# A hybrid encoder with 2 x 32 experts on one core: TensorE's order in the experts changed so that a down product stands behind the next expert's gate and up product

## What is computed

```python
def run(args):
    xe, e_i = args
    hdn = jax.nn.silu(xe @ w_gate[e_i]) * (xe @ w_up[e_i])
    return hdn @ w_down[e_i]
...
contrib = yb[dest].astype(F32) * sg[:, None]
return jnp.zeros((T, d), F32).at[stok].add(contrib).astype(xt.dtype)
```

## Time and profile before

| | |
|---|---|
| median of 3 runs | 1803.88 us (1802.73 to 1806.07) |
| profiled execution: its time, its span | 1805.69 us, 1803.8 us |
| TensorE busy | 1589.4 us (88%) |
| VectorE, ScalarE, POOL busy | 695.3, 435.6, 194.1 us |
| granted TensorE clock, mean | 0.973 |
| experts of layer 0, first gate and up product to last down product | 411.2 to 896.7 us |
| experts of layer 1, the same | 1287.0 to 1775.3 us |

### The profile page before, as it was taken

One profiled execution on the slowest core, in us unless ns is written; L12 is line 12 of the kernel. 1 busy time (PEld: TensorE's weight loads), 2 busy tenths in 40 slices (PEclk: granted clock), 3 DMA queues, 4 the chain that ended last, 5 costly groups with the idle time before them and its releaser, 6 DMA issues.

```text
span 1803.8 us, 22591 instructions
## 1 busy us (share of the span) xinstructions
PE 1589.4 (88%) x7494; PEld 763.4 (42%) x7494; DVE 695.3 (39%) x1432; ACT 435.6 (24%) x989; POOL 194.1 (11%) x199
## 2 busy tenths in 40 slices
PE   5999998998998998787889999999899988887883
PEld 2455645453333343333345555455333333333331
DVE  1677576352222112222157855743422222222124
ACT  2111567112111112111121016742111221111111
POOL 0000022111111011111000002101111111111010
PEclk9999999989999999999999999999999999999997
DMA  9625533079999999999972355212799999999994
GB/s 362 231 70 202 195 115 110 17 293 398 407 401 407 408 408 404 417 410 417 365 298 93 122 204 208 68 48 101 290 400 407 403 409 406 411 416 404 399 395 180
DMA packets 118493, 527.56 MB, mean 292 GB/s; under 512 B 16529, under 2 KB 22673, under 8 KB 69265
## 3 DMA queue, kind: packets, MB, share of 16 engines
q1 hardware_dynamic: 100944, 491.49, 69.0%
q0 software_dynamic: 12496, 24.51, 4.2%
q10 hardware_dynamic: 4976, 10.55, 1.6%
HBM read 520.99 MB, written 23.86 MB: 302 GB/s over the span
## 4 chain that ended last, share of the span: by engine, by line
PE 56%; DMA 27%; SPq 6%; DVE 5%; issue 3%; ACT 3%; POOL 1%; ACTq 0%; DVEq 0%; POOLq 0%
DMA ring<-in_w_exp_up 20%; PE ps L1015 18%; PE ps L1373 17%; PE ps L1228 6%; SPq L841 5%; PE ps L1371 4%; DMA hT<-in_w_exp_up 3%; PE ps L1170 2%; PE ps L1184 2%; PE ps L1210 2%; PE ps L1041 1%; DMA ring<-in_w_in 1%; ACT arena L1664 1%; DMA yexp_d<-arena,masks 1%; PE ps L1404 1%
## 5 line engine op out<-in xcount | busy, mean ns | idle before, releaser
L1373 PE MATMUL ps<-ring,arena 128*64 128x512 f32 x1952 | 589.1, 603 | 59.2 <-ACT arena L1664 35.0
L1373 PEld LDWEIGHTS ps<-ring,arena 128*64 128x64 f32 x1952 | 184.8, 138 | 273.5 <-issue 260.2
L1015 PE MATMUL ps<-ring,hT 128*128 128x512 f32 (+1 forms) x768 | 255.0, 487 | 1.5 <-DVE z L1804 0.9
L733 DVE TENSOR_TENSOR arena<-ps,arena 64x512 f32<-64x512 f32 (+1 forms) x64 | 44.3, 693 | 488.6 <-ACT arena L1658 418.6
L1658 ACT ACTIVATE arena<-ps 128x512 f32<-128x512 f32 x64 | 38.2, 597 | 778.9 <-PE ps L1373 724.3
L1015 PEld LDWEIGHTS ps<-ring,hT 128*128 128x128 f32 x768 | 144.4, 191 | 101.5 <-issue 91.2
L1373 PE MATMUL ps<-home,arena 128*64 128x512 f32 x320 | 148.6, 619 | 24.2 <-DMA ring<-in_w_exp_up 20.5
L1373 PE MATMUL ps<-hT,arena 128*64 128x512 f32 x336 | 151.5, 605 | 6.9 <-DMA ring<-in_w_exp_up 6.9
L980 POOL DMA_INDIRECT yexp_d<-arena,masks x64 | 59.3, 927 | 850.3 <-DVE arena L743 772.9
L741 DVE TENSOR_TENSOR arena<-ps,gate 64x512 f32<-64x512 f32 (+1 forms) x64 | 43.7, 683 | 266.2 <-PE ps L1373 246.6
L1228 PE MATMUL ps<-ring,hT 128*128 128x512 f32 x256 | 112.5, 595 | 0.0
(11 more groups left out here) (218 smaller groups left out, 1645.2 us busy)
## 6 DMA issues: line engine op xcount, KB each, us to landing
ring<-in_w_exp_up SPq DMA_DIRECT2D x108, 1024.0 KB
ring<-in_w_exp_down SPq DMA_DIRECT2D x88, 1024.0 KB
ring<-in_w_exp_gate SPq DMA_DIRECT2D x62, 1024.0 KB
ring<-in_w_ada SPq DMA_DIRECT2D x24, 2048.0 KB, 11.1
home<-in_w_exp_gate SPq DMA_DIRECT2D x44, 1024.0 KB
work<-in_w_exp_down SPq DMA_DIRECT2D x40, 1024.0 KB
hT<-in_w_exp_gate SPq DMA_DIRECT2D x22, 1024.0 KB
hT<-in_w_exp_up SPq DMA_DIRECT2D x20, 1024.0 KB
```

What stands on the lines that cost most here:

```text
L1015: last = pe.matmul(out, lhs(k), rhs(k), start=(k == 0), stop=(k == n - 1))
L1373: last = [pe.matmul(outs[c][HALF * c:HALF * c + HALF, :], lhs(k)[:, 0:HALF], rhs(c, k), start=(k == 0), stop=(k == n - 1), tile_position=( ...
```

## The change

On TensorE, the body of the loop was: turned product rows of k, down product of k, gate and up product of k+1, turned tokens of k+2. It becomes: gate and up product of k+1, turned tokens of k+2, down product of k, turned product rows of k+1. On VectorE, the scaling of the down product's rows of k moves behind the tokens of k+2.

```diff
@@ experts_dve
             expert_tokens(0, 0)
             expert_hidden(0, 0, 0)
             expert_tokens(1, 1)
-            expert_rows(0, 0, 0)
             expert_hidden(1, 0, 1)
             expert_tokens(2, 0)
-            expert_rows(1, 0, 1)
+            expert_rows(0, 0, 0)
             expert_hidden(2, 1, 0)
             expert_tokens(3, 1)
+            expert_rows(1, 0, 1)
             with dve.Fori(1, HE - 1) as it:
-                expert_rows(2 * it, it, 0)
                 expert_hidden(2 * it + 1, it, 1)
                 expert_tokens(2 * it + 2, 0)
-                expert_rows(2 * it + 1, it, 1)
+                expert_rows(2 * it, it, 0)
                 expert_hidden(2 * it + 2, it + 1, 0)
                 expert_tokens(2 * it + 3, 1)
+                expert_rows(2 * it + 1, it, 1)
@@ TensorE
                 gate_up(0, 0)
                 turn_tokens(0, 1)
+                turn_hidden(0, 0)
                 with pe.Fori(0, NE // 6) as q:
                     for n in range(6):
-                        turn_hidden(q, n)
-                        down(q, n)
                         gate_up(q, n + 1)
                         turn_tokens(q, n + 2)
-                turn_hidden(NE // 6, 0)
+                        down(q, n)
+                        turn_hidden(q, n + 1)
                 gate_up(NE // 6, 1)
                 down(NE // 6, 0)
```

## The result

The changed kernel takes 1986.78 us in the median of 4 runs (1981.56 to 1991.38), against 1804.62 us (1802.73 to 1806.07, 4 runs) for the kernel before: a ratio of 1.1005, with a 95% interval of 1.0978 to 1.1033. The forecast was slower, 1928 us, with a range of 1864 to 1966: the direction and the loop that causes it hold, the size is 59 us too small and outside the range.

What follows compares the result with a forecast made beforehand. Before, weights bound at 15.7 us per expert, with TensorE's 13.7 us pace early in each stage; after, a gather loop of 16.0 us. 1803.9 + 61.5 (loop, wide experts, stage ends) + 62 (clock) gave about 1928 us, range 1864 to 1966.

Steps and rivals of the forecast that it cites:

- step 2: Expert loop: tokens gathered behind the scatter come late, TensorE waits 3.2 us each step, giving 16.0 us per expert.
- F + 3.55: POOL's issue of the gather three experts ahead, 3.55 us after F, the end of an expert's down product.
- step 6: TensorE's clock falls after three quarters of the gather waits, 1.5 us each over 55 loops: 62 us, bounds 0 and 83.
- step 2's 7.5 us: Time from the gather's issue to its rows landing with DMA engines full, taken from the old order's 7.4 and 7.5.
- work costed at nothing: VectorE's later row scaling and SP's down places freed 8 us later, claimed free since weights come three experts early.
- the wide experts: Three experts, two in layer 0 and one in layer 1, with longer products: some 9 us extra each.
- A: Rival: gather in time, DMA stream sets the end, late release costs +5 to +12 us, 1809 to 1816; chance 0.08.
- B: Rival: gathers land within 4.3 us, quicker steps put more places in flight earlier, 8 us faster, 1796; chance 0.04.
- D: Rival: the gather loop is longer still, a 9 us landing adding 87 us, over 1970; chance 0.08.

Runs made afterwards that it cites:

- e7: Changed kernel with only SP's weight loads reordered, gate and up of the next expert ahead of down of this one; 1901.49 us, ratio 1.0546.
- e2: Changed kernel plus four products of constants on TensorE between the gate and up product and the turned tokens; 1909.99 us, ratio 1.0602.
- e9: Changed kernel with SP's loads as in e7 and the filler of e2, with three products of constants instead of four; 1873.81 us, ratio 1.0376.
- e1: Changed kernel with POOL issuing the gather three experts ahead before the scatter instead of behind it; 1816.14 us, ratio 1.0071.
- e3: Changed kernel with the down product ahead of the turned tokens, and VectorE's scaled rows moved ahead likewise; 1817.11 us, ratio 1.0079.
- e10: Kernel before, TensorE and VectorE in old order, with POOL's gather of two experts ahead put behind the scatter; 2046.97 us, ratio 1.1317.
- e4: Changed kernel with each weight load after the first nine cut to a quarter of its half, timing only; 1695.2 us, one run.
- e5: Kernel before with each weight load after the first nine cut to a quarter of its half, timing only; 1733.57 us, one run.
- e6: Changed kernel with the gather ahead of the scatter as in e1 and SP's loads in TensorE's new order; 1803.75 us, ratio 0.9999.
- e8: Kernel before with only POOL's edit of e1, the gather three experts ahead issued before the scatter; 1802.27 us, ratio 0.9982.

## Why the prediction was right in kind and too small in size

The table has means over those narrow steps in which TensorE waited for the gather, in us, worked out from the timeline rows of TensorE and POOL (51 steps of the changed kernel, 449.24 to 1927.37; 51 of e7; 40 of e2; 46 of e9).

| | forecast | changed | e7 | e2 | e9 |
|---|---|---|---|---|---|
| gather's issue to turned tokens | 7.64 | 8.20 | 7.05 | 8.64 | 7.82 |
| turned tokens | 1.16 | 1.82 | 1.53 | 1.15 | 1.15 |
| down product | 3.65 | 5.03 | 4.66 | 3.65 | 3.69 |
| wait ahead of the turned tokens | 3.2 | 4.07 | 2.93 | 0.88 | 0.94 |
| steps with a slow down product | 3 in 4 | 51 of 51 | 39 of 51 | 0 of 40 | 1 of 46 |

**The loop (step 2).** Right, and shown, with a step of 18.6 us where I had said 16 to 17.5. It closes through down product, scaled rows, scatter, gather, turned tokens: F + 3.55 for the issue is what the timeline after has, 54 waits stand at L1352, and each way of opening the loop (e1, e3) gives 1816 to 1817 us. e10 makes it without the change.

**The clock (step 6).** This is the step that failed, the term that was mis-sized. I took three waits in four to be followed by the low level, at 1.5 us each, 62 us. The granted clock was 0.50 in the stretch from 504 to 508, and 0.86 over 450 to 570, where I had said 0.90 to 0.96. The down product was slow in all 51 steps and the turned tokens in 47 of them, in the mean by 1.38 + 0.66 = 2.04 us: 51 x 2.04 = 104 us, 42 more than forecast. Both factors were too low. My 1.5 came from one gate and up product behind a wait of 2.46 us. My share came from the waits of the kernel before, and it was too low even for a wait of the size that I forecast. In the changed kernel the 7 waits of 1.74 to 3.3 us were all followed by the low level, like the 44 longer ones. In e7, 10 of the 11 waits of 3.0 to 3.3 us were, and all 17 longer ones. That e7 comes to 39 of 51, close to my three in four, is the work of its short waits: of the 17 under 2.5 us only 7 were. Length alone doesn't decide it: in the kernel before, TensorE kept its clock behind the wait of 3.04 us in the earlier trace rows.

**The landing (step 2's 7.5 us).** This is the second term that was mis-sized: 8.20 us to the turned tokens instead of 7.64, 0.56 x 51 = 29 us. I took the landing from the old order as a constant, although I had seen it go from 3.8 to 10.8. e7 shows that it depends on the order of the loads around it. Under "work costed at nothing" I wrote that the later release of places costs nothing here, since the weights come early; the weights did, but all five halves went out at the moment of the gather. e7 shows what that was worth: with the loads moved, landings are 1.15 us shorter to the turned tokens and the whole kernel 85 us faster, by way of the clock as well.

**The rest.** The 58 steps from the first to the 30th scatter of each layer last 541.7 and 539.5 us, 18.6 each; the forecast's were (482 + 473 + 62) / 58 = 17.5. The two terms above come to 71 us over the forecast and this difference to 64. By the ends of the down products in the timeline, the 51 narrow steps that waited lasted 18.5 us in the mean, 72 over the forecast's 17.1. The other seven (three with a wide gate and up product, 18.9 each; three with a wide down product, 21.7 to 22.8; the last of layer 1) lasted 135.8 us where I had charged 143.5. More than half of this difference is that last step: it took 12.4 us and waited for no gather. The rest is the wide experts, which I overcharged a little.

Two of my readings were loose, and neither moves the forecast. The DMA line stands at 9 from the tenth slice on, not from the ninth (7, 293 GB/s). And 1803.9 + 61.5 gives 1865 for the lower end of the range, not 1864.

**The rivals.** A's price, 5 to 12 us, was a microsecond too low for e1 (13), but A needs a landing of at most 4.3 us, and the median here was 8.1. The rule of the Trainium skill for a transfer from GpSimd (DMA: Bandwidth & Descriptors, Anatomy of one DMA) gives an estimate of 2.6 us and would have made A the result. The traces don't agree: 8.1 us with the weights beside it, and still 4.7 and 3.5 with a quarter of them (e4, e5). B did not come: e6 has everything that B asks for, steps of 12.4 us and places released early, and stands at 0.9999. The time fell where D put it, over 1970, not by a landing of 9 us but by clock and landing together. The kernel that the Trainium skill tells of (TensorE: Matmul & The Clock Gate, HAM oscillation), whose clock fell at every such wait, was the better guide in the point where I departed from it: here too it fell at each of the 51. Its price, 0.83 us for each, was too low for this kernel, where it was 2.04.

**What stays open.** What besides its length decides whether a wait brings the low level. Why landings differ between e7 (7.2) and e9 (7.4 in the median, 7.8 to the turned tokens in the mean) is argued from the DMA rates; no run holds the traffic fixed and changes the moment of the gather alone. Why e8 is 0.18% faster was not looked into.

## What to carry to other kernels

Before moving a product on one engine, follow what its end releases on the other queues, and measure the way from that release back to the same engine: if a transfer stands in it, its latency is part of the step as soon as the new order needs the data within one step. In a queue in order, a load that is needed soon must not stand behind a store that waits for the engine (e1: three lines, 170 us of 182). And a latency read in one order is not a constant of the other: ask what else is issued at that moment, and what an engine's wait does to its clock, before the terms are added.

## What the hardware showed that I had not expected

The same kernel became 77 us faster by 480 added matmul instructions that nobody reads (7974 against 7494), since they kept TensorE's clock at 2.4 GHz through a wait (granted 1.00 over 440 to 900, where the changed kernel has 0.88). A gather of up to 64 rows took 3.5 us in the median with weight loads of a quarter the size beside it, 7.4 with the whole ones, and 8.1 with five halves of 1 MB issued just ahead of it.
